# A recurrence in chunks of 64: each head in its own 64x64 quarter of the array

## The reference, cut to what matters

```python
def _rwkv7_step(S, inp):
    r, w, k, v, kk, a = inp
    sa = jnp.einsum('bhvk,bhk->bhv', S, kk)
    S = S * w[:, :, None, :] - sa[..., None] * (kk * a)[:, :, None, :] + v[..., None] * k[:, :, None, :]
    y = jnp.einsum('bhvk,bhk->bhv', S, r)
    return S, y
...
    S0 = jnp.zeros((B, RWKV_HEADS, HEAD_DIM, HEAD_DIM), jnp.float32)
    _, y = lax.scan(_rwkv7_step, S0, (tm(rh), tm(decay), tm(kh), tm(vh), tm(kk), tm(ah)))
```

## Time and profile before

| | us |
|---|---|
| median of 3 runs | 2444.24 |
| lowest and highest run | 2438.68, 2444.53 |
| the profiled execution, its own time | 2448.63 |
| its span in the trace | 2446.9 |
| PE busy | 2273.7 (93%) |
| DVE busy | 1444.0 (59%) |
| ACT busy | 1065.0 (44%) |
| POOL busy | 1090.1 (45%) |

### The profile page before, as it was taken

One profiled execution on the slowest core, in us unless ns is written; L12 is line 12 of the kernel. 1 busy time (PEld: TensorE's weight loads), 2 busy tenths in 40 slices (PEclk: granted clock), 3 DMA queues, 4 the chain that ended last, 5 costly groups with the idle time before them and its releaser, 6 DMA issues.

```text
span 2446.9 us, 47596 instructions
## 1 busy us (share of the span) xinstructions
PE 2273.7 (93%) x17599; PEld 2225.5 (91%) x17599; DVE 1444.0 (59%) x2872; ACT 1065.0 (44%) x1739; POOL 1090.1 (45%) x537
## 2 busy tenths in 40 slices
PE   7878699998999999999998787899999999999999
PEld 6867699998999999999988776898899999999999
DVE  2773415997667755555546834329906777555555
ACT  4522245664333344444444312356663333444444
POOL 4794056887566610000016980378976666000000
PEclk9856799999999999999999756899999999999999
DMA  4200034443444445555544000255454444555554
GB/s 153 78 1 1 8 129 157 163 163 129 134 133 137 130 157 176 171 175 176 172 145 139 1 1 1 71 180 163 163 180 139 144 138 145 173 188 181 187 182 169
DMA packets 88288, 320.28 MB, mean 131 GB/s; under 512 B 9744, under 2 KB 11024, under 8 KB 87824
## 3 DMA queue, kind: packets, MB, share of 16 engines
q1 hardware_dynamic: 88208, 319.24, 39.2%
HBM read 318.15 MB, written 1.05 MB: 130 GB/s over the span
## 4 chain that ended last, share of the span: by engine, by line
PE 55%; POOL 23%; issue 20%; DVE 1%; ACT 0%; POOLq 0%; DMA 0%; SPq 0%; DVEq 0%
PE ps L813 55%; POOL w_lo L508 13%; POOL arena L529 6%; POOL arena L538 3%; DVE h L1608 0%; DMA w<-w_c 0%; POOLq L514 0%; DVE x L1218 0%; POOL arena L525 0%; POOLq L507 0%; DVE x_lo L1211 0%; DVE sel L1520 0%; ACT arena L604 0%; DVE onehots_j L1206 0%; PE ps L1138 0%
## 5 line engine op out<-in xcount | busy, mean ns | idle before, releaser
L813 PE MATMUL ps<-x_hi,w_hi 128*128 128x272 f32 (+1 forms) x6816 | 1543.0, 287 | 43.2 <-POOL w_lo L508 27.7
L813 PE MATMUL ps<-x_hi,w_lo 128*128 128x272 f32 (+1 forms) x4768 | 1360.7, 285 | 0.0
L508 POOL TENSOR_TENSOR w_lo<-w,w_hi 128x1024 fp32r<-128x1024 f32 x344 | 863.3, 2519 | 975.2 <-ACT w_hi L586 974.9
L813 PEld LDWEIGHTS ps<-x_hi,w_hi 128*128 128x128 f32 x6816 | 1150.1, 189 | 51.6 <-POOL w_lo L508 34.2
L813 PEld LDWEIGHTS ps<-x_hi,w_lo 128*128 128x128 f32 x4768 | 899.7, 189 | 0.0
L586 ACT CAST w_hi<-w 128x1024 fp32r<-128x1024 f32 x596 | 623.0, 1046 | 446.2 <-DMA w<-v_c 393.2
L813 PE MATMUL ps<-x_lo,w_hi 128*128 128x272 f32 (+1 forms) x2720 | 775.7, 285 | 0.0
L813 PEld LDWEIGHTS ps<-x_lo,w_hi 128*128 128x128 f32 x2720 | 514.8, 189 | 0.2
L1590 DVE TENSOR_TENSOR w_lo<-w,w_hi 128x1024 fp32r<-128x1024 f32 x252 | 308.8, 1225 | 342.1 <-ACT w_hi L586 342.1
L813 PE MATMUL ps<-arena 128*128 128x64 f32 (+9 forms) x1448 | 274.1, 366 | 74.3 <-ACT arena L617 15.8
L813 PEld LDWEIGHTS ps<-arena 128*128 128x128 f32 (+6 forms) x1448 | 244.8, 253 | 100.1 <-issue 30.9
(11 more groups left out here) (157 smaller groups left out, 1534.9 us busy)
## 6 DMA issues: line engine op xcount, KB each, us to landing
w<-u_c SPq DMA_DIRECT2D x256, 512.0 KB, 3.3
w<-v_c SPq DMA_DIRECT2D x256, 512.0 KB, 3.2
w<-w_c SPq DMA_DIRECT2D x84, 512.0 KB, 3.3
arena<-keys_c SPq DMA_DIRECT2D x2, 1024.0 KB, 5.6
arena<-mix_c SPq DMA_DIRECT2D x2, 792.0 KB, 7.1
h<-h SPq DMA_DIRECT2D x1, 1088.0 KB, 5.1
out<-h SPq DMA_DIRECT2D x4, 256.0 KB, 2.3
arena<-lora_c SPq DMA_DIRECT2D x2, 256.0 KB, 7.2
```

What stands on the lines that cost most here:

```text
L508: g.tensor_tensor(wlo_t[:, slot], wraw_t[:, slot], whi_t[:, slot].bitcast(F32), ALU.subtract).then_inc(s_lo, 1)
L813: return nc.tensor.matmul(out_, lhsT, rhs, start=start, stop=stop, skip_group_check=True)
```

## The change

The products no longer use all of the array. For each head half `r` in `HALVES` (partitions 0 to 63 and 64 to 127) there is a matmul of its own, with its 64 rows of the stationary and the moving operand in partitions `r`, and its result in PSUM partitions `r`; so head 0 of a tile uses one 64x64 quarter of the array, and head 1 the quarter diagonally opposite. The two follow each other in the program. What was one 128x128 product is now two of 64x64, and the block-diagonal copies are gone, on ACT and on DVE. The token-major "transposes" are now ordinary float32 matmuls against a quarter of the identity, and a chunk's six results fit into one bank, so that four banks take turns. State, X and U are 64 columns per head pair instead of 128. The masks `mT` are half as wide, so `mix_c` shrinks by 320 columns. PE's waits on `s_dg` and `s_g0` become waits on `s_fm` and `s_grc`.

```diff
+HALVES = (slice(0, HD), slice(HD, P))
...
-            def blocks(dst, src):
...
-                for i, (src, dst) in enumerate(((t3, v_d), (be, be_d), (ka, ka_d))):
-                    act.wait_ge(s_fm, 3 * l + i + 1)
-                    blocks(dst.rearrange("p j c t -> p (j c) t"),
-                           src.rearrange("p j (c t) -> p (j c) t", c=NCH)).then_inc(s_dg, 1)
...
-                        nc.scalar.copy(xm[:, j], src)
-                        blocks(xm_d[:, j], src).then_inc(s_xc, 1)
+                        nc.scalar.copy(xm[:, j], src).then_inc(s_xc, 1)
...
-                    if c >= 2:
-
-                        pe.wait_ge(s_tmc, l * NCH + c - 1)
-                    for m, src in enumerate((v_d, ka_d, be_d)):
+                    if c >= 4:
+
+                        pe.wait_ge(s_tmc, l * NCH + c - 3)
+                    w = slice(c * CHUNK, (c + 1) * CHUNK)
+                    for m, src in enumerate((t3, ka, be)):
                         for j in range(2):
-                            last = nc.tensor.transpose(ps[:, 3 + 2 * (c % 2) + m // 2,
-                                                          (2 * (m % 2) + j) * P:(2 * (m % 2) + j + 1) * P],
-                                                       src[:, j, c, :], ident)
+                            for r in HALVES:
+                                last = mm(ps[r, 3 + c % 4, (2 * m + j) * HD:(2 * m + j + 1) * HD], src[r, j, w],
+                                          ident[r, r], True, True)
...
+                def product(bank, a, b_, j):
+
+                    for c in range(NCH):
+                        for r in HALVES:
+                            last = mm(ps[r, bank, c * CHUNK:(c + 1) * CHUNK], a[r, j, c, :], b_[r, j, c, :], True, True)
+                    return last
...
-                        for c in range(NCH):
-                            last = mm(ps[:, 3 + j, c * CHUNK:(c + 1) * CHUNK], cm_d[:, j, c, :], ti[:, j, c, :],
-                                      True, True)
-                        last.then_inc(s_x, 1)
+                        product(3 + j, cm, ti, j).then_inc(s_x, 1)
...
-                                       bc(gram[:, :, j, 2, :], 2, 2),
-                                       bc(mT[:, b].rearrange("p (q t) -> p q t", q=2), 1, NCH), ALU.mult)
-
-            def tt_diag(j):
...
+                return v.tensor_tensor(cm[:, j], gram[:, :, j, 2, :], bc(mT[:, b], 1, NCH), ALU.mult)
...
-                link(v.tensor_tensor(al_d.rearrange("p j c (q t) -> p (j c) q t", q=2),
-                                     bc(al.rearrange("p j (c t) -> p (j c) t", c=NCH), 2, 2),
-                                     bc(blk.rearrange("p (q t) -> p q t", q=2), 1, 2 * NCH), ALU.mult))
...
-                    v.tensor_copy(flat(xs), ps[:, 3, 0:2 * P]).then_inc(s_xs, 1)
+                    v.tensor_copy(flat(xs), ps[:, 3, 0:P]).then_inc(s_xs, 1)
```

More of the change, by code:

```diff
@@ L149, in constants @@
     put("negm1T", both(-1.0 * cross(1, t, s)))
-    put("mT", np.stack([np.kron(np.eye(2), cross(b, t, s)) for b in LEVELS[1:]], 1))
+    put("mT", both(np.stack([cross(b, t, s) for b in LEVELS[1:]], 1)))
     put("distM", np.abs(np.arange(NMETA)[:, None] - np.arange(NMETA)[None]))
@@ L280, in trunk @@
         t1, t2, t3 = two(), two(), two(TP)
-        state = A.take(2 * 2 * P).rearrange("p (b j n) -> p b j n", b=2, j=2)
+        state = A.take(2 * P).rearrange("p (b j n) -> p b j n", b=2, j=2)
         B = Arena(cat_t, 4 * T)
-        decayed, xs, us = (B.take(2 * P).rearrange("p (j n) -> p j n", j=2) for _ in range(3))
+        decayed, xs, us = (B.take(P).rearrange("p (j n) -> p j n", j=2) for _ in range(3))
         over = A.at
@@ L295, in trunk @@
         over_prep = A.at
[L298 to L305, removed]
         A.at = over_prep
-        be_d, ka_d = diag(A.take(DIAG)), diag(A.take(DIAG))
-        A.at = matrices
         gram = A.take(NCH * 2 * 4 * CHUNK).rearrange("p (c j m t) -> p c j m t", c=NCH, j=2, m=4)
-        cm_d, tt_d, xm_d = (diag(A.take(DIAG)) for _ in range(3))
-        vkb = A.take(NCH * 3 * 2 * P).rearrange("p (c m j n) -> p c m j n", c=NCH, m=3, j=2)
+        cm = A.take(2 * TP).rearrange("p (j c t) -> p j c t", j=2, c=NCH)
+        vkb = A.take(NCH * 3 * 2 * HD).rearrange("p (c m j n) -> p c m j n", c=NCH, m=3, j=2)
         vtok, ktok, btok = (vkb[:, :, m] for m in range(3))
-        g0_d = v_d
         ti, tt_, xm = (a.rearrange("p j (c t) -> p j c t", c=NCH) for a in (be, ka, t3))
@@ L708, in _ @@
                 after(steps)
-                act.wait_ge(s_grc, NCH * (l + 1))
-                blocks(g0_d, gram[:, :, :, 0, :].rearrange("p c j t -> p j c t")).then_inc(s_g0, 1)
                 for b in range(len(LEVELS) - 1):
@@ L1052, in _ @@
                     if c < NCH - 1:
-                        for j in range(2):
-                            last = mm(ps[:, 5, jw(j, P)], btok[:, c, j, :], us[:, j, :], False, True)
-                        last.then_inc(s_cs, 1)
-                    for j in range(2):
-                        last = mm(ps[:, yb, jw(j, CHUNK)], us[:, j, :], gram[:, c, j, 3, :], False, True)
-                    last.then_inc(s_cy, 1)
+                        pairs(5, lambda r, j: btok[r, c, j, :], lambda r, j: us[r, j, :], False,
+                              True).then_inc(s_cs, 1)
+                    pairs(yb, lambda r, j: us[r, j, :], lambda r, j: gram[r, c, j, 3, :], False,
+                          True).then_inc(s_cy, 1)
                     after(steps)
```

74 lines of the change are left out of this document (30 added, 44 removed).

## The result

The changed kernel takes 2380.59 us (median of 4 runs, 2375.99 to 2382.72) against 2441.46 (4 runs, 2438.39 to 2444.53) of the kernel before on the same chip: the comparison gives a ratio of 0.9725, with a 95% interval of 0.9701 to 0.9749. The profiled execution has a span of 2377.0 us; before it was 2446.9.

What follows compares the result with a forecast made beforehand. It took the inverse to be bound by PE at 1.2 GHz, except its first level, by DVE. Per layer 6.5 + 21 + 2 + 4 = 33.5 us, twice 67, plus 0.4: 2444.2 - 67.4 = 2376.8 us, range 2355 to 2400 (8 in 10: 2340 to 2434).

Steps and rivals of the forecast that it cites:

- The price of a pair: PE matmuls: two 64x64 records run together, costing 0.107 us at the low clock and 0.053 at the high one.
- First level, 6.5 us a layer: Inverse, first level: DVE drops four operations of line 1232 (4.0 us) and halves four of line 1226 (2.5 us).
- Levels two to five, 21 us (15 to 28): Inverse, later levels: 230 records cost PE 49.5 us; pairs take off 24.7, of which 21 counted per layer.
- the attention's shadow: Later levels: part of PE's gain lost where attention on ACT and DVE comes last; lower bound 15 us.
- Transposes and gram, 2 us: Before the inverse: transposes gain 1.1 us and gram 1.3, less 0.4 for tile shape changes, per layer.
- State, 4 us a layer: State stage: a 4.18 us chunk becomes 3.0 at the high clock or about 3.8 at the low; 6 or 2 us.
- Start, 0.4 us: Kernel start: PE's wait for the last load shortens with 160 KB less to load, 0.5 us at most.
- Stage lengths: Profile after: the two inverses near 71 and 89 us, the state stages near 43 and 23.
- (C): Rival: quarters take turns, so the change saves copies and no matmul time; 2435 us, chance 0.17.
- (D): Rival: quarters take turns and the clock falls to 1.2 GHz in transposes, gram and state; 2474 us, chance 0.05.
- (B): Rival: the clock rises in the inverse, 22 us per layer more gained; 2333 us, chance 0.10.
- POOL: POOL's convolution, ending at 1458.4 us, would still be some 29 us early with 30 us taken from the second mixer.

Runs made afterwards that it cites:

- e1: Changed kernel with both matmuls of every pair in the same quarter (rows and columns 0 to 63): 2469.24 us, 1.0089 of the kernel before.
- e4: Nine rows of 24 zero matmuls added after the first squares; 48 records took 2.74 us in one quarter (line 898), 1.45 diagonally by turns into one bank (901).
- e3: Changed kernel with the levels' five matmuls of the first quarter before the five of the second, instead of by turns: 2398.95 us, 0.9796 of the kernel before.
- e2: Changed kernel with the levels' block-diagonal copies on DVE and ACT back, matmuls still in quarters: 2400.63 us, 0.9802 of the kernel before.
- e6: Changed kernel with 36 instead of 48 products of zeros before the transposes: 2372.42 us, 0.9696 of the kernel before.
- e5: Changed kernel with products of zeros added in the levels, 6 after X's products and 16 at each level's end: 2387.28 us, 0.9752 of the kernel before.
- e7: Changed kernel with the attention's norm moved out of the first level, its reciprocals before the gram's masks: 2361.52 us, 0.9648 of the kernel before.

## Why the prediction was right, point by point

- **The price of a pair** (0.107 us at the low clock, 0.053 at the high one) was the step on which all hung, and one that the trace of before could not show for one PSUM bank. Measured: 0.115 and 0.060, 8 and 13% more. That loads and products of both quarters run together is shown by e1 and by e4's lines 898 and 901. But its support in the earlier trace rows, "even from a program order that doesn't alternate", fails for longer groups: e3 and line 907. Had the products of the levels been written that way, the change would have brought 17 us less.
- **First level, 6.5 us a layer.** Measured 5.5 (29.7 to 24.2), and 4.9 came back in e2. The sum had the right operations with prices that were partly POOL's. Its mean of 1.26 us for line 1226 holds two of 1.84 and 1.96 us in the first layer's set-up, each of which ended 0.68 us after an addition of POOL that it ran into; the other two took 1.77 together. After the change line 1341 runs into POOL in their place. So line 1226 gave 3.1 us instead of 2.5, line 1232 gave 3.5 instead of 4.0, and line 1341 took 1.9 back.
- **Levels two to five, 21 us (15 to 28).** Measured 68.7 - 45.0 = 23.7 in the first layer, and the inverse of the second layer shrank by 28.6, nearly as much. The sum counted 230 records; the last level has no T·X, so they are 3 x 60 + 40 = 220, 47.3 us, and half of that is 23.7 instead of 24.7. It then took 3.7 off for the attention's shadow, and 21 came out 2.7 too small. Either less lay in the shadow, or the clock, which rose from 0.52 to 0.65 here, made up for it; no run separates the two. Nor is 2.7 much: the changed kernel run again takes 42.0 us for this stretch instead of 45.0. In e1 the stretch is 19.0 us longer than in the changed kernel, in e2 6.5 us. The sum had put no gain to the copies apart from PE's, because they lie behind PE and "would be next": e2 shows what that means, since with the copies in place PE's halved time would have been worth 6.5 us less.
- **Transposes and gram, 2 us.** Measured 1.7. A gram chunk takes 0.69 + 0.41 = 1.10 us (forecast 1.07), the transposes 3.58 (3.2). What the sum had at nothing, the zeros in front, became the bound: DVE is done at 110.7 us, they end at 112.3, and in e6's profile the transposes come 1.3 to 1.6 us sooner with fewer of them.
- **State, 4 us a layer** as a mean of 6 and 2. Measured 2.3 and 8.9. The chunk of 2.91 us at clock 1.00 (forecast 3.0) is right. The second layer gained more than 6 with a clock that rose from 0.89 to 1.00, and the first stayed near 2 with one that fell from 0.82 to 0.72; in the second profile of the changed kernel it is 0.79 and the stage takes 42.1 us. The sum of 11.2 beside the 8 forecast is thus partly luck with the clock.
- **Start, 0.4 us.** Measured 0.43 (14.15 instead of 14.58).
- **Stage lengths.** Inverses 69 and 88 us (71 and 89 forecast), state 44.5 and 18.1 (43 and 23).
- **What was missed:** 3 us lost behind the first mixer, where the granted clock dips; its cause stays open. The forecast's 67.4 us stand beside 69.9 of the span, which are 72.8 of gains less 3.
- **The rivals.** (C), taking turns because of the bank, is refuted by lines 901 and 904. Its price of 2435 us was too kind: e1 shows 2469. (D) named both the price and the clock of 0.50 in the state. It had the gram's clock wrong, and its sum too: the 10.7 us for the gram are 5 x 2.14 at the high clock, and at 1.2 GHz they would be twice that, so that its 2474 lies near the measured 2469 by luck. (B) came in a small way: 0.53 to 0.64 and 0.51 to 0.61 in the inverse, where I had argued from the gapless stretch at 0.50 that it would not rise.
- **POOL.** 1458.4 us is the start of the convolution's last step; it ends at 1459.8, still early enough.

## What to carry to other kernels

Where a matmul's operand is half zeros, look at what its rows and columns cost to load: two matmuls in separate quarters take about half the time of the one they replace (0.115 us a pair of records instead of 0.215), if their order in the queue alternates and both start from data that lies in the right partitions. Cost such a change by PE's own time at the clock that the stage has, and then look for what stands right behind it, here copies on two engines which were over a quarter of the gain. When a stage stops being PE's, the next gain lies in whatever an engine does in line without need: here a norm, moved to where its engine waited, was worth 16 us, and moving it one step further was worth nothing, since the next to wait stood there.

## What the runs showed of the hardware that I had not expected

- Same rows, different columns: two quarters fed from the same 64 rows, 48 records in 1.34 us against 2.74 for one quarter.
- Overlap reaches only a few records ahead in the queue: 24 records of one quarter before 24 of the other saved 0.35 us, about six records of 0.057; ten before ten, at the low clock, saved 0.37 us (2.21 to 1.84), about three of 0.11.
- The granted clock of a stage did not follow from PE's gaps in it. It was 0.64 with PE busy for 39 of 69 us (inverse, changed kernel), 0.53 with 73 of 98 (before) and 0.50 with 56 of 64 (levels two to five, e1); but with zeros between the products it was 0.89 with 42 of 50 (levels two to five, e5). In the first layer's state it was 0.72 with the pairs and 0.50 with serial quarters. What decides it these runs don't show.
- A DVE operation on `arena` that begins while POOL adds can stretch until just after POOL's end: 0.35 us after it for 320 elements, in six of six cases in the set-up of the first layer (changed kernel, e6, e7), on two different operations, 1.02 to 1.65 us instead of 0.49 to 0.66. No run moved POOL's work to test it.
